# Two-layer hybrid encoder block: the order of high and low weight pieces in the wide experts' gate and up products

## The reference

```python
def swiglu(u, wg, wu, wd):
    return (jax.nn.silu(u @ wg) * (u @ wu)) @ wd

def moe_swiglu(h, w_router, b_router, w_gate_e, w_up_e, w_down_e):
    t = h.reshape(n, d)                                    # n = 256, d = 1024
    logits = (t @ w_router) + b_router
    top_val, top_idx = lax.top_k(logits, TOP_K)            # 2 of 8
    gates = jax.nn.softmax(top_val, axis=-1)
    ...
    def expert_block(args):                                # e's rows, padded to blocks
        xblk, e = args
        return swiglu(xblk, w_gate_e[e], w_up_e[e], w_down_e[e])   # 1024 x 3584, twice, and 3584 x 1024
    ...
    y = jnp.zeros((n, d)).at[tok_sorted].add(yb[dest] * g_sorted[:, None])
```

## Time and profile before

| | |
|---|---|
| time, median of 3 runs | 1860.13 us (1859.55 to 1861.48) |
| the profiled execution's own time | 1856.83 us |
| its span, first to last instruction | 1854.8 us |
| granted TensorE clock, mean of the span | 0.909 of full speed |
| PE busy | 1610.9 us (87%) |
| PEld busy | 1301.3 us (70%) |
| DVE busy | 711.0 us (38%) |
| ACT busy | 549.7 us (30%) |
| experts with the 160 body | one, about 1249 to 1434 us |
| experts with the 192 body | one, about 1530 to 1731 us |

### The profile page before, as it was taken

One profiled execution on the slowest core, in us unless ns is written; L12 is line 12 of the kernel. 1 busy time (PEld: TensorE's weight loads), 2 busy tenths in 40 slices (PEclk: granted clock), 3 DMA queues, 4 the chain that ended last, 5 costly groups with the idle time before them and its releaser, 6 DMA issues.

```text
span 1854.8 us, 30986 instructions
## 1 busy us (share of the span) xinstructions
PE 1610.9 (87%) x12674; PEld 1301.3 (70%) x12675; DVE 711.0 (38%) x1019; ACT 549.7 (30%) x752; POOL 63.3 (3%) x67
## 2 busy tenths in 40 slices
PE   3899997999999999976666799998998758999894
PEld 2777775999997677755444588547987548888552
DVE  1134216455532342141000588116775015666212
ACT  1122104333321231020000576106554005544201
POOL 0000000000001000010000000000000000000002
PEclk8998788999999987788777899999999878999998
DMA  6733345654435133267999999999667898655794
GB/s 221 278 125 148 136 159 216 260 187 185 174 126 197 57 148 136 91 249 304 419 421 420 421 418 376 407 421 398 253 252 283 348 419 333 246 217 216 278 422 176
DMA packets 76975, 488.83 MB, mean 264 GB/s; under 512 B 12096, under 2 KB 16460, under 8 KB 18956
## 3 DMA queue, kind: packets, MB, share of 16 engines
q1 hardware_dynamic: 71616, 478.02, 64.2%
q10 hardware_dynamic: 4620, 6.41, 1.1%
q0 software_dynamic: 576, 2.10, 0.3%
HBM read 482.56 MB, written 3.93 MB: 262 GB/s over the span
## 4 chain that ended last, share of the span: by engine, by line
PE 79%; DMA 7%; issue 5%; DVE 3%; ACT 2%; ACTq 2%; POOL 1%; SPq 0%; POOLq 0%; DVEq 0%
PE PG L1260 9%; DMA ring<-in_experts 6%; PE Y L886 5%; PE PG L1304 4%; PE PG L1370 4%; PE Y L1272 4%; PE TRB L1304 4%; PE Y L1332 4%; PE Y L894 3%; PE Y L1143 3%; PE PG L850 3%; PE PG L851 3%; PE PG L852 3%; PE TRB L1310 3%; PE PG L1310 3%
## 5 line engine op out<-in xcount | busy, mean ns | idle before, releaser
L1260 PE MATMUL PG<-ring,mixT 128*32 128x128 f32 (+1 forms) x1920 | 119.2, 356 | 61.6 <-issue 61.6
L1453 ACT ACTIVATE parts<-ring 128x2048 fp32r<-128x2048 f32 x84 | 158.4, 1904 | 13.0 <-PE Y L852 8.3
L1260 PEld LDWEIGHTS PG<-ring,mixT 128*32 128x32 f32 (+1 forms) x1920 | 91.7, 141 | 91.4 <-issue 76.0
L2245 DVE COPY arena<-TRB 128x64 f32<-128x64 f32 (+1 forms) x70 | 17.6, 251 | 346.0 <-PE TRB L1245 346.0
L1453 ACT ACTIVATE rope<-PG 64x128 f32<-64x128 f32 (+2 forms) x84 | 27.3, 325 | 381.3 <-PE PG L1260 358.3
L1260 PE MATMUL PG<-arena,mixT 128*32 128x128 f32 (+1 forms) x1664 | 105.1, 362 | 39.9 <-issue 39.9
L850 PE MATMUL PG<-h_parts,parts 128*128 128x256 f32 x448 | 128.2, 286 | 10.2 <-DVE parts L2121 10.2
L1260 PEld LDWEIGHTS PG<-arena,mixT 128*32 128x32 f32 (+1 forms) x1664 | 82.2, 144 | 67.9 <-issue 54.7
L851 PE MATMUL PG<-h_parts,parts 128*128 128x256 f32 x448 | 128.0, 286 | 0.0
L852 PE MATMUL PG<-h_parts,parts 128*128 128x256 f32 x448 | 127.9, 285 | 0.0
L2121 DVE TENSOR_TENSOR parts<-ring,parts 128x2048 fp32r<-128x2048 f32 x42 | 95.9, 2292 | 25.7 <-ACT parts L1453 25.5
(11 more groups left out here) (378 smaller groups left out, 2949.2 us busy)
## 6 DMA issues: line engine op xcount, KB each, us to landing
ring<-in_experts SPq DMA_DIRECT2D x168, 1024.0 KB, 13.5
arena<-in_experts SPq DMA_DIRECT2D x168, 1024.0 KB, 17.2
ring<-in_weights SPq DMA_DIRECT2D x116, 1024.0 KB, 5.9
ring<-in_weights SPq DMA_DIRECT2D x4, 512.0 KB, 4.1
ypairs<-hT ACTq DMA_DIRECT2D x3, 512.0 KB, 5.3
tok<-in_x ACTq DMA_DIRECT2D x1, 1024.0 KB, 13.9
result<-scr SPq DMA_DIRECT2D x2, 512.0 KB, 2.6
ring<-in_weights SPq DMA_DIRECT2D x2, 432.0 KB, 6.7
```

Of the source, the lines that this page charges most:

```text
L1260: last = mm(bank[i * n:(i + 1) * n, 0:width], xe[:, k, 0:n], w[k // 4][:, k % 4, i * width:(i + 1) * width], start=(k == 0), stop=(k == KD ...
L1453: return nc.scalar.activation(out_, in_, func, **kw)
```

## The change

Inside a half stage of `expert_wide`, PE now takes the high and the low matmul of the same 128 x 128 block one after the other, bank by bank. The wait for the low piece (`lo_ready`) stands in front of the half, beside that for the high piece, and `hi_used` is raised by the last high matmul, which is now the last but one of the half. No instruction of another engine changes.

```diff
                     hi_ready(e, q)
+                    lo_ready(e, q)
                     for i, bank in enumerate(banks):
                         both = bank[:, 0:2 * n].rearrange("p (v t) -> p v t", v=2)
                         for k in range(KD // 2):
-                            last = mm(both, hi[:, k, i // 2, i % 2, :], h_parts[:, :, h * KD // 2 + k, 0:n],
+                            high = mm(both, hi[:, k, i // 2, i % 2, :], h_parts[:, :, h * KD // 2 + k, 0:n],
                                       start=(h == 0 and k == 0), stop=False, skip_group_check=True)
-                    last.then_inc(hi_used, 1)
-                    lo_ready(e, q)
-                    for i, bank in enumerate(banks):
-                        for k in range(KD // 2):
                             last = mm(bank[:, 0:n], lo[:, k, i // 2, i % 2, :], h_parts[:, 0, h * KD // 2 + k, 0:n],
                                       start=False, stop=(h == 1 and k == KD // 2 - 1), skip_group_check=True)
+                    high.then_inc(hi_used, 1)
```

## The result

| | before | changed |
|---|---|---|
| median | 1860.13 us (1859.18 to 1863.06, 11 runs) | 1866.21 us (1864.36 to 1873.12, 11 runs) |
| ratio | | 1.0038, 95% interval 1.0025 to 1.0051 |
| profiled execution | 1856.83 us, span 1854.8 | 1864.36 us, span 1862.6 |

The forecast was 1845.5 us, in a range of 1839 to 1852. The change made the kernel 6.1 us slower instead of some 15 faster.

The account below looks back on a forecast made before the run. PE was taken to bound the two wide experts. Steady stages save 10.1 us (n=160) and 7.5 (n=192), the starts cost 3.2, net 14.4 us less: 1845.5 us from the median 1860.1, range 1839 to 1852.

Parts of the forecast that it names:

- the price of a pair: One high plus one low matmul at n=160: 0.257 us before, 0.222 alternating, saving 0.48 us a half stage.
- the 10.1 and the 7.5 us of the forecast: Savings over 13 steady stages each: 0.78 us a stage at n=160, 0.58 us at n=192.
- my two bounds: Pair at n=160: 0.216 us if loads never bind, saving 0.57 a half stage; 0.257 if order does not matter, saving nothing.
- The moved wait at the start: At each wide expert's start PE waits uncovered for DVE's low piece, starting 2.34 us later at n=160.
- 0.4 us of it would come back in the first half: First half at n=160 takes 5.6 us against 6.02, with 4.1 us at 1.2 GHz; stage 0 ends 1.5 us later.
- For n=192 I had 1.7: Start of the n=192 expert: 2.34 us late less 2 x 0.29 saved, so stage 0 ends 1.7 us later.
- The wait in the steady stages: At n=160 PE waits about 0.18 us for DVE's low piece once a stage; at n=192 none.
- The banks' wait at stage 1: PE's wait for the banks after stage 0 of the n=160 expert, 1.9 us in the kernel before.
- Rivals 2 and 3: DVE becomes the bound at n=160, 1850.5 us, chance 0.12; DMA takes back the n=160 gain, 1854 us, chance 0.05.
- Rival 1: Loads overlap only partly, so order does not matter (pair 0.257 us) and both starts pay: 1864.8 us, chance 0.07.

Follow-up runs that it names:

- e5: Kernel before (16 high, then 16 low matmuls), low ones cut to 64 of 128 stationary columns, half the low product left out: 1837.70 us, ratio 0.9881.
- e3: Kernel before (16 high, then 16 low matmuls), low ones cut to 64 moving columns, rest of low product left out: 1864.33 us, ratio 1.0010.
- e6: Changed kernel (alternating), low matmuls cut to 64 of 128 stationary columns, half the low product left out: 1866.26 us, ratio 1.0045.
- e4: Changed kernel (alternating), low matmuls cut to 64 moving columns, rest of low product left out: 1883.92 us, ratio 1.0118.

## Why the prediction was wrong

**The step that failed** is in the price of a pair: "So a low matmul itself needs 0.07 us, and 0.04 us of each 0.111 is waiting for the loader, which in the high block has ... 0.035 us to spare each time and cannot bank it. Alternating gives each low matmul that spare time." The first half is true: the low stream needs 0.07 and e5 shows it at 0.073. The second is not. The 0.07 between the first low matmul and the second was read as a low step without a wait. It is the distance of two starts, and a start is noted before the weights are complete; the wait was there, a step later, and nothing was saved over the whole. e3 shows this directly, with 0.02 for a first step whose stream is 64 columns, and so does the changed kernel's 0.19 behind each 0.07. A load is not hidden by the matmul two ahead, only by the one just ahead. The loader's spare 0.035 us beside a high matmul cannot be used, since the next load begins only with the next matmul's stream. So the sum of the longer ones is right, 0.146 + 0.111 = 0.257, and not the longer of the sums, 0.222. This took away the 10.1 and the 7.5 us of the forecast: 13 stages each gave -1.0 and +0.8 us. Between my two bounds the answer was the one I set aside: the measured pair is 0.26.

**What held.** PE was the bound. The moved wait at the start: 2.34 us late was forecast, 2.42 measured at n=160 (PE starts 0.14 us behind DVE's end and not 0.07). That 0.4 us of it would come back in the first half was wrong. That half took 6.51 us in the changed kernel, from 1260.01 to the first matmul of the second at 1266.52, against 6.02; at 1.2 GHz its pairs were 0.48 us apart and not 0.444, for some 5.0 us and not 4.1 (the half's granted clock was 0.61: 0.39 x 6.51 / 0.5 = 5.1). So stage 1 starts 3.05 us late where I had 1.5. For n=192 I had 1.7; it was 4.5 at stage 1, and 2.9 by stage 2, because the kernel before spent part of its stage 1 at 1.2 GHz (15.6 us instead of 13.95). The wait in the steady stages never came, because its premise, a shorter half stage, did not. The banks' wait at stage 1 stayed at 2.0 us. Rivals 2 and 3 had nothing to act on.

**The rivals.** Rival 1 (0.07) had the price, 1864.8 against 1866.2, and the place, the two starts. Its mechanism was half right: the order does not matter, but not because loads overlap only partly. They overlap fully with the matmul ahead. The Trainium skill's rule ("TensorE: Matmul & The Clock Gate", section "The mechanism"), that a load overlaps matmuls in flight only with other rows, is not what the runs show if it is taken alone. The same section also lets a load into the background weight buffer run ahead of matmuls in flight, and I left that half out. The runs do not show which buffer a load goes to, but they agree with that half: in the earlier trace rows a load of 0.111 us over all rows hides behind each high matmul of 0.146, and in e5 a shorter one behind each low matmul of 0.073.

I gave it 0.07 because one number, the first low matmul's 0.07 us, spoke against it, and the whole gain of the forecast hung on the same number. The bound of 0.257, where the order does not matter, stood in the text and needed no such reading.

## What to carry to other kernels

Where weights are loaded one ahead, price a sequence of matmuls step by step, each the longer of its own stream and the next load. By this rule, if all loads are equally long, no order of long and short matmuls gains anything (here it made 0.08 us more in a stage of 12 and 0.06 less in one of 14, which nothing explains yet); if they differ, put the short loads together behind short streams, as the 24 us of stages between e5 and e6 show. And before interleaving two products that wait for different producers, look at the first pass: the later producer's lead is hidden in the steady state and uncovered at every start.

## What the runs showed of the hardware that was not expected

- The start of a matmul in the trace comes before its weights are complete. Behind a long matmul the next distance reads 0.07 us (160 columns), 0.09 (192), or about 0.03 (64, in e3 and e4), where the step costs 0.111.
- In e4, long and very short matmuls in turn, the clock granted behind an expert's start stayed at 1.2 GHz much longer: 0.63 in the window from 1260 to 1300 us against 0.94 in the changed kernel, with PE busy 34.79 of the 40 us. Its two wide experts are 17 us longer than the changed kernel's, with the same waits at the start (9.8 us and 2.0) and steady stages within 0.05 us, so the difference is clock. In e3 the same matmuls in groups had 0.81 in that window. What decides it was not tried.
